# Two thirds of a gated unit moved between expert operations, and its weights through a ring of buffers

## What is computed

```python
def s5_mixer(u, ...):                       # width 1024
    ...                                     # a linear scan gives y
    g = jax.nn.gelu(y)
    out = g * jax.nn.sigmoid(g @ w_glu)     # the gated unit

def mamba2_mixer(z, xbc, ...):              # width 1024
    ...
    y = y * jax.nn.silu(z)                  # the gate
    yg = y.reshape(bsz, L, M2_GROUPS, M2_WIDTH // M2_GROUPS)
    yg = yg * lax.rsqrt(jnp.mean(yg * yg, axis=-1, keepdims=True) + EPS)
    y = yg.reshape(bsz, L, M2_WIDTH) * norm_w

def decoder_layer(x, ...):
    ...
    y_s5 = rmsnorm(y_s5, s5_norm_w)
    x = x + jnp.concatenate([y_s5, y_m2], axis=-1) @ w_out
    x = x + peer_ffn(rmsnorm(x, norm_ffn_w), w_q, sub_keys, u_tab, v_tab)

def peer_ffn(h, w_q, sub_keys, u_tab, v_tab):
    q = (h @ w_q)                           # queries, 1024 x 2048
    ...                                     # scores, two times top 16, softmax g: 128 experts a token
    act = gelu(sum(u_tab[idx] * h))
    return sum((g * act) * v_tab[idx])
```

## Time and profile before

| what | value |
|---|---|
| median of three runs | 4100.95 us (4100.71 to 4111.82) |
| the profiled execution | 4114.0 us |
| its span in the trace | 4112.2 us |
| busy PE, DVE, ACT, POOL | 2647.1, 2369.4, 1191.5, 1364.7 us |
| bytes moved | 1295.60 MB, 315 GB/s in the mean |

### The profile page before, as it was taken

How to read it: one execution, slowest core, us unless ns; L and a number is a source line. 1 busy time by engine, 2 the same in 40 slices (tenths; PEclk the granted TensorE clock), 3 DMA queues, 4 the chain that set the end, 5 groups by cost and what they waited for, 6 DMA issues and landing times.

```text
span 4112.2 us, 47318 instructions
## 1 busy us (share of the span) xinstructions
PE 2647.1 (64%) x16198; PEld 1290.2 (31%) x16198; DVE 2369.4 (58%) x4875; ACT 1191.5 (29%) x2967; POOL 1364.7 (33%) x1291
## 2 busy tenths in 40 slices
PE   7999835989585677775474474474465455556444
PEld 4556724545362222233141141141131122123110
DVE  2354193752155854447667557657657757747754
ACT  2011111212112344432333333333333333333332
POOL 4000010310003443343444444444444444444433
PEclk9999966989796779887585585585576576567555
DMA  3311213430527999999999999999999999999998
GB/s 117 76 68 65 84 24 111 118 115 28 200 90 316 423 426 401 386 414 394 374 426 426 422 426 426 412 424 426 423 409 426 423 411 426 427 408 426 426 420 360
DMA packets 275693, 1295.60 MB, mean 315 GB/s; under 512 B 47152, under 2 KB 109872, under 8 KB 134192
## 3 DMA queue, kind: packets, MB, share of 16 engines
q0 software_dynamic: 156672, 1140.92, 66.3%
q1 hardware_dynamic: 118736, 151.16, 11.5%
HBM read 1246.26 MB, written 43.36 MB: 314 GB/s over the span
## 4 chain that ended last, share of the span: by engine, by line
DMA 43%; PE 12%; issue 7%; DVE 5%; ACT 4%; POOL 1%; POOLq 0%; SPq 0%; DVEq 0%; ACTq 0%
DMA pe_ring<-in_uv,pe_index_now 39%; PE pe_ps_q L1800 4%; PE pe_acc L1872 4%; DVE pe_ring L1733 3%; PE pe_ps_q L1835 2%; DMA pe_shared<-scratch_s_t 1%; DMA pe_w_q<-in_w_q 1%; PE pe_ps_t L1865 1%; ACT pe_mark L1526 1%; POOL pe_ring L1431 1%; DMA scratch_x_mid<-pe_shared 1%; ACT pe_weight L1528 1%; ACT L1526 1%; DVE pe_shared L1571 1%; DMA pe_ring<-in_w_q 1%
## 5 line engine op out<-in xcount | busy, mean ns | idle before, releaser
L1733 DVE CUSTOM_DVE_ANT_0 pe_ring<-pe_ring,pe_h_rep 128x1024 f32<-128x1024 f32 x1088 | 1327.8, 1225 | 903.3 <-DMA pe_ring<-in_uv,pe_index_now 848.8
L1431 POOL DMA_INDIRECT pe_ring<-in_uv,pe_index_now x1088 | 1227.4, 1128 | 1508.7 <-PE pe_acc L1872 1358.6
L1872 PE MATMUL pe_acc<-pe_ring,pe_weight 128*32 128x256 f32 x8704 | 987.1, 544 | 1147.0 <-ACT pe_weight L1528 1142.6
L1526 ACT ACTIVATE pe_mark<-pe_eye,pe_dot 128x32 f32<-128x32 f32 x1088 | 349.2, 321 | 1674.5 <-DVE pe_dot L1733 1673.0
L1872 PEld LDWEIGHTS pe_acc<-pe_ring,pe_weight 128*32 128x32 f32 x8704 | 207.8, 129 | 1898.1 <-ACT pe_weight L1528 1791.4
L1528 ACT ACTIVATE pe_weight<-pe_mark,pe_gate_now 128x32 f32<-128x32 f32 x1088 | 349.5, 321 | 35.1
L558 PE MATMUL pj_bank<-pj_x_t,pj_w_buf 128*128 128x512 f32 (+1 forms) x960 | 316.5, 492 | 2.7 <-DVE pj_x_t L419 2.7
L1835 PE MATMUL pe_ps_q<-pe_shared,pe_w_q 128*128 128x128 f32 x1792 | 252.6, 299 | 24.3 <-DMA pe_w_q<-in_w_q 24.3
L1835 PEld LDWEIGHTS pe_ps_q<-pe_shared,pe_w_q 128*128 128x128 f32 x1792 | 230.3, 208 | 74.9 <-issue 60.4
L1800 PE MATMUL pe_ps_q<-pe_w_q,pe_shared 128*128 128x512 f32 x448 | 234.7, 649 | 0.0
L558 PEld LDWEIGHTS pj_bank<-pj_x_t,pj_w_buf 128*128 128x128 f32 x960 | 158.7, 193 | 155.8 <-issue 154.3
(11 more groups left out here) (300 smaller groups left out, 2710.3 us busy)
## 6 DMA issues: line engine op xcount, KB each, us to landing
pe_ring<-in_uv,pe_index_now POOLq DMA_INDIRECT x1088, 15.4
pe_ring<-in_w_q SPq DMA_DIRECT2D x8, 2048.0 KB, 11.6
pj_w_buf<-in_w_in SPq DMA_DIRECT2D x13, 1024.0 KB, 6.2
pe_w_q<-in_w_out SPq DMA_DIRECT2D x2, 4096.0 KB, 17.5
pe_w_q<-in_w_q SPq DMA_DIRECT2D x4, 2048.0 KB, 44.4
scratch_xbc<-pj_z_out SPq DMA_DIRECT2D x12, 552.0 KB, 4.4
m2s_xbc<-scratch_xbc SPq DMA_DIRECT2D x8, 768.0 KB, 5.1
pj_early<-in_x_all SPq DMA_DIRECT2D x9, 512.0 KB, 3.6
```

The costliest lines, as they stand in the source:

```text
L1431: nc.gpsimd.indirect_dma_start(out=ring[:, p, :], out_offset=None, in_=D["uv"], in_offset=bass.IndirectOffsetOnAxis(ap=row, axis=0)).then_ ...
L1526: A(mark[:, p, :], eye[:], ACT.Gelu_apprx_tanh, scale=dot[:, p:p + 1]).then_inc(mark_ready, 1)
L1733: V.tensor_tensor_reduce(out=ring[:, p, 0:D_MODEL], in0=ring[:, p, 0:D_MODEL], in1=h_rep[:, g % 2, :], scale=1.0, scalar=0.0, op0=ALU.mult ...
L1872: last = T.matmul(acc[j * PER:(j + 1) * PER, g % 2, 0:COLS], lhs(j), src[:, j * COLS:(j + 1) * COLS], start=first, stop=final)
```

## The change

`mix_out` keeps only the declaration of `scratch_s5_t`. The gated unit is computed in `route_and_experts`:

- Its operands lie in one tensor, `early_space`, which takes over the roles of `w_q` and `w_out` when the last group has been computed.
- The first part (eight groups) stands at the start. Beside its groups the gates of Mamba's tiles 0 to 6 are computed, with a sigmoid and two products in place of the Silu; tiles 7 and 8 follow behind it (`LATE_GATES`). The gated tiles 2 to 8 are stored to DRAM over `ym` and loaded again when they are mixed.
- The two other parts (16 groups) are computed in steps 0 to 38 of tile 0's experts, as half groups of four products on PE in four of five steps (`GLU_HALVES`); sigmoid, product, squares, sum, root and norm follow some steps later.
- Tiles 0 and 1 multiply with `w_out` in pieces of 2 MB, which come through the two buffers in the ring with the query pieces (`PIECES`, sixteen in all). The first quarter of tile 1's product stands ahead of tile 0's routing on PE. `w_out` is loaded once more as a whole at steps 39 and 51.
- Mixing of tiles 2 to 8 starts later in the table (59 to 161 in place of 28 to 158), takes 25 steps in place of 34, and its loads go out a tile ahead. `w_q` is loaded again in two halves.
- POOL's waits for the end of tile 1's scores and queries stand ahead of the third and the fifth gather in place of the first.

The diff, cut:

```diff
-        w_q = sb("w_q", [P, KT, PAIR * P])
+        w_q = early["space"][:, 0:KT * PAIR * P].rearrange("p (c n) -> p c n", c=KT)
+        w_out = early["space"][:, 0:2 * KT * D_MODEL].rearrange("p (c n) -> p c n", c=2 * KT)
...
-    MIX_AT = {2: 28, 3: 66, 4: 84, 5: 103, 6: 121, 7: 140, 8: 158}
+    GLU_HALVES = {i * 5 // 4: i for i in range(2 * (PARTS - 1) * KT)}
+    GLU_END = {KT + i // 2: s for s, i in GLU_HALVES.items() if i % 2}
+    GLU_SIG, GLU_GATE, GLU_SQUARE, GLU_SUM, GLU_ROOT, GLU_NORM = 1, 2, 2, 3, 4, 6
+    GATES, LATE_GATES = {c: (c - 1,) for c in range(1, KT)}, (KT - 1, KT)
+    PIECES = [("out", 8), ("out", 12), ("out", 0), ("out", 4), ("out", 8)] + [("q", n) for n in range(PAIR // 4)] + \
+             [("out", 12), ("out", 0), ("out", 4)] + [("q", n) for n in range(PAIR // 4)]
+    MIX_AT = {2: 59, 3: 76, 4: 93, 5: 110, 6: 127, 7: 144, 8: 161}
...
+            def piece_load(i):
                 if i >= 2:
-                    sp.wait_ge(q_made, i - 1)
+                    sp.wait_ge(*piece_done(i - 2))
...
+            sp.wait_ge(s5_ready, KT)
+            for b in BLOCK_0:
+                s5_store(0, b, lambda m: s5_1_out if m == 1 else s5_0_out)
+            piece_load(2)
+            gate_store(TILES - 2)
+            piece_load(3)
...
+                if s == last + 1:
+                    sp.wait_ge(glu_made, KT * PARTS)
+                    sp.dma_start(w_out[:, 0:KT], D["w_out"][:, KT:]).then_inc(w_out_in[1], 16)
+                if s == last + GLU_NORM + 7:
+                    sp.dma_start(w_out[:, KT:], D["w_out"][:, 0:KT]).then_inc(w_out_in[0], 16)
...
-            pool.wait_ge(q_made, EARLY * UNITS)
-            pool.wait_ge(x_in, 16 * EARLY)
-            pool.wait_ge(h_ready, EARLY)
-            pool.wait_ge(score_moved, 1)
+            pool.wait_ge(x_in, EARLY * 16)
...
             def background(s):
-                for m in range(TILES - 1, EARLY - 1, -1):
-                    mix(m, s - MIX_AT[m])
                 r, g = routed(s)
                 if r == 2 or g >= EXP:
                     route(r, g, r)
+                for C in glu_steps(s, GLU_SQUARE):
+                    glu_square(C)
+                for C in glu_steps(s, GLU_SIG):
+                    glu_sig(C)
...
+            for c in range(KT):
+                for half in range(2):
+                    glu_half(c, half)
+                if c:
+                    glu_sum(c - 1)
+                if c in (5, 7):
+                    turn_m2(c // 2 - 2)
+            glu_sum(KT - 1)
+            for j in range(4):
+                early_out(0, j)
+            early_out(1, 0)
             for g in range(CHOICE):
                 route(0, g, False, 0)
```

603 lines of the change are left out of this document (372 added, 231 removed).

## The result

The changed kernel takes 4048.2 us (median of four runs, 4042.5 to 4053.3) against 4100.8 before (median of four), so 52.6 us less; the ratio of the means is 0.9865, interval 0.9844 to 0.9886. Forecast were 4039 and 62 us less. In later jobs the kernel before took 4103.6 to 4106.5, so by medians the gain is 53 to 58 us. The profiled execution took 4042.5 us, its span is 4040.7.

What follows compares the result with a forecast made beforehand. Order of work bounds the front, bytes the experts. Front -120 us and experts +58 (41 + 23 - 6) take the 4100.95 median to 4039 us; range 3995 to 4080.

Steps and rivals of the forecast that it cites:

- the forty steps: Tile 0's first forty expert steps, with sixteen groups among them: 142 us against 101, excess 41, ends 0 and 60.
- (1): Front: two thirds of the gated unit leave the chain ahead of the first gather, 103.65 us less.
- (2): PE's start on the gated unit: constants behind four 512 KB loads, 10 us against 2.2; loss 8, between 2 and 12.
- (3): Gated unit's first third: sixteen transposes between groups lose 3 us with a cold start; Mamba's gates beside them cost nothing.
- (4): From the end of the gated unit's groups to x of tile 0: 46.4 us in place of 75.8, gain 29.
- (5): From x of tile 0 to its queries: 13 us in place of 7.3, loss 6, up to 12.
- (6): Queries, still through two refilled buffers, now with sixteen pieces: zero change, within 10 us either way.
- (7): Product of tile 1: 27.63 us becomes three quarters, 20.7, plus a wait of 3 for a piece; gain 4.
- Bytes and stalls: After the first gather: 23 us more for net bytes and later loads, less 6 gained where mixing waited.
- A: Rival: the stream of gathers hides the moved groups, so the steps have no excess; total 3998 us, chance 0.20.
- B: Rival: the weight pieces become the chain in front, whose gain is only 85 us; total 4074 us, chance 0.13.
- C: Rival: low PE clock in expert steps with groups, forty steps take 226 us; total 4123 us, 0.5% slower, chance 0.09.

## Why the prediction was right, and where not

The time lies in the range and the mechanism is the one that was forecast: a chain in front loses the groups, the steps that take them in become slower than the gathers, and the first is worth more. The kernel with the groups in front shows it alone: 58.9 us. That the total came within 10 us of the forecast is in part luck: the ring cost 34.5 us that nothing in the working stood for, and the front and the stretch behind the forty steps gained about as much more than forecast. Against the steps of the working:

- (1) holds: 103.65 us were taken out; with norms and stores it is 116.7.
- (2) PE's start: 903.14 - 894.82 = 8.3 us after the first load, against 2.2: loss 6, taken as 8. (3) From there to the eighth sigmoid 47.2 us against 46.3, loss 1, taken as 3; the gates did lie beside the groups.
- (4) 950.30 to 995.77 is 45.5 us, forecast 46.4; the wait for the third piece is in it, as said. (5) 11.5 us to the queries, forecast 13.
- (6) and (7) 1007.30 to 1068.78 is 61.5 against 69.3 before: gain 8, taken as 4. (8) 53.7 against 54.2.
- Together -131, within the bound of -140, where -120 was taken: three small losses were taken some 2 us too large each, and the gain of (7) 4 too small.
- The forty steps: 42.4 us of excess, forecast 41, but by errors that cancel. The table's wait is 1.2 us in five steps in place of 2.3, as the load ahead of the sigmoid lies in ACT's wait. (The working's own terms, 15.1 + 2.3 + 0.5, give 17.9 for five steps and not 17.5.) The wait of VectorE for a store was not counted: 10.60 us, worth 13.2. The changed program has that wait (the last channel's norm waits for `first_out`), and the working does not name it; the upper end of 60 alone stood for it. And forty steps of the kernel before take 105.9 and not 101: the working stretched the first 32, and the mixing of tile 2 begins at step 28.
- Bytes and stalls: +17 forecast, -0.8 measured from the 41st product to the seed of tile 2, and 5 of that is the ring, so about -6. The bytes cost what they should, less a fifth; so the gain where the mixing waited was not the 6 that were taken but over 20. The term was read from 100 us with one such wait, and the mixing goes on through most of the stretch. Behind these items stand its windows, before and then changed, and the two largest waits for loads other than gathers in it, of the kernel before (us in total, times, longest). At 425 GB/s the bytes of this stretch would have taken 39 us less before, and at 419 some 17 us less after: 22 us of loss went. Neither of the two waits is left in the changed kernel; what each was worth was not tried apart.
- Missing altogether: the ring's start, +34.5 by the kernel with the ring moved. The prediction treated the allocation as neutral, and its sentence that time in the stream falls only when bytes fall is too strong: with the same bytes the last stretch took 2097.9 us in place of 2128.9.

```profile
1380.00:2013.00 633.00, 450.54 (x2613) 172.58 (x2613) 368.07 (x731) 227.98 (x557) 262.29 (x218) 0.80 0.98 399
```

```profile
1280.00:1911.00 631.00, 450.12 (x2622) 168.65 (x2614) 369.23 (x725) 185.34 (x497) 265.62 (x219) 0.81 0.99 408
```

```profile
ACT pe_shared L1455 <- DMA pe_shared<-scratch_s_t: 37.6, 4, 12.1
PE pe_ps_q L1835 <- DMA pe_w_q<-in_w_q: 24.3, 2, 14.0
```

Without the ring's loss the change gives 4013.7, a gain of 87 us and 25 more than forecast; with it the gain is 9 less than forecast. So the sum is right in its main terms and helped by errors of both signs: front and stalls were better than taken, the ring and VectorE's wait worse.

Of the rivals, A fails (the steps take 148.3 us with the groups and 100.6 without, and with a quarter of the products they are 23 us shorter, so the stream did not hide them), B has a small part (5.4 us at the first gather when one piece comes earlier), C did not happen: the granted clock in the steps was 0.94, as the evidence of 0.90 said. The DMA share there is 0.88 and not 0.7, though 324 of some 420 GB/s are 0.77: a share near 0.9 was not yet a full stream.
